# Splitting x without its row factors, in a hybrid attention and retention layer

## The chip, the cores and the metric

One core of a Trainium2 chip runs the whole layer. The metric is device time of one execution in microseconds (us). TensorE multiplies matrices, VectorE, ScalarE and GpSimd work on elements, SyncE issues all DMA transfers. The pages of the profile call them PE (its weight loads PEld), DVE, ACT, POOL and SP (SPq where it issues a transfer).

## What is computed

x is 2048 rows by 1024 columns of float32. The reference, shortened (the chunk-wise retention is given in its effect: sums over decayed keys inside a chunk, a state R across chunks):

```python
h = x * rsqrt(mean(x*x, axis=-1) + 1e-6) * norm_gain      # one factor per row, one gain per column
aq, ak, av, ag, rq, rk, rv, rg = split(h @ w_in, SPLIT_POINTS, axis=-1)

# group A: 16 heads of 64, 4 KV heads, window of two chunks of 64 rows
q, k = rms_norm(aq, q_norm_gain), rms_norm(ak, k_norm_gain)      # per head
s = q @ k.T / 8 + bias                                           # ALiBi, band of 128 keys
p = exp(s - m) / (sum(exp(s - m)) + exp(sink - m))
attn = p @ av

# group B: 8 heads, q and k of 64, v of 128, decay g per head
o = ((rq @ rk.T) * dmat) @ rv + (rq * wq) @ R                    # R: g**64 * R + (rk * wk).T @ rv
ret = (o - mean(o)) * rsqrt(var(o) + 1e-6) * ret_norm_gain       # per head and row

mixed = concatenate([attn * silu(ag), ret * silu(rg)], axis=-1)
out = x + mixed @ w_out
```

The projection w_in has 5632 columns, w_out is 2048 by 1024.

## The kernel before

**Tiling.** The rows are taken in four blocks of 512 (BLK, four tiles of 128, t = 0 to 3). A block has four units (NU), one for each KV head: four attention heads with their key and value, and two retention heads. So there are 16 units n, unit 0 to 3 on the first block, and so on. All matrix products are made of float32 operands that are split in two, high + low, with three matmuls for each pair (high x high, high x low, low x high; `mm3` and `job`, L1327 to L1329). A high half is a copy that rounds (ScalarE), a low half is the original minus the high half.

**Jobs of TensorE.** Unit n has jobs (n,0) to (n,19). Jobs 0 to 3 are q, k and v of a row tile (24 matmuls with 384 columns, panel 0 of the weights), 4 and 5 the attention gate, 6 and 7 retention q and k (24 matmuls with 512 columns each, weights stationary, so the result has features as rows: panel 1), 8 to 11 retention v and gate of a row tile (panel 2), 12 to 19 the output projection (12 matmuls with 512 columns each, panel 3), done while the next unit starts. Results land in three PSUM banks jb in turn; job m waits until the reader of the job three before has freed its bank. Between the jobs stand short pieces: TQ(n,t) transposes the normed q and k of a tile, S_ makes scores, PT transposes probabilities, PV multiplies with v, A and I are the retention products, MT transposes the mixed result, XB (L1443) transposes the row factors of x.

**x.** A transposed tile of x (features as rows) comes from DRAM into one of two buffers xt (x_turned, L253). For it the row factor is needed along the columns: xsq (ScalarE, a sum of squares from a row-major copy: acc in the first block), xms_ (VectorE, L1028, mean and eps), xpow (GpSimd, L401, power -0.5), XB (TensorE, one factor column spread over 128 and transposed). h (VectorE, L1042) scales xt in place by gain and factor, eight instructions of 128x128 per tile; in block 0 the factor is read from the PSUM bank of XB, later from xrb in SBUF (buffer rawqn). xh (ScalarE, L648) makes the high halves hTH, two copies of 128x512 per tile. The low halves hTL come from VectorE in block 0 (xl_first, through `sub`, L804) and from GpSimd in later blocks (xl, L408). For block b + 1 h of the first two tiles stands in the middle of the last unit of block b, the rest of it at that unit's end. x_turned of tile t waits for the low halves of tile t - 2, whose buffer it takes.

**Weights.** In the first block a panel is read in four pieces of 128 x 2 slices (load q) into three stages; wh1 (ScalarE, L508) makes each slice's high half, wl1 (GpSimd, L360) the low half; both halves are saved to scratch in DRAM and later blocks reload them (reload), without splitting. SyncE issues each piece's load when the low halves of the piece three before are done, and that piece's save right behind it.

**After the jobs.** qkv (ScalarE) copies the q, k, v bank to raw. VectorE and GpSimd norm q and k (rpow, L367, is the power). ag and agg are the attention gate: tanh from the bank (ScalarE), then (tanh + 1) x bank on VectorE (L914) into gate, which frees the bank. rq_decay, rk, rvg, kw_am (L959, L960), rl and rupd (L979) are retention, gna, gnv, gnb the group norm, mix, mixh, mixl, mtl the mixed result, add the residual. carry_in brings keys and values of the block before, negates the sinks (L820) and copies the retention state rst to rcur.

**Order.** Each engine runs a list of such calls, written out by hand for every unit; semaphores alone order the engines among each other. The start of the lists of TensorE and GpSimd:

```python
XB(0, 0)
job(0, 0); job(0, 1); TQ(0, 0); job(0, 2); TQ(0, 1); S_(0, 0); job(0, 3); job(0, 4); TQ(0, 2)
...
xpow(0, 0); wl1(0, 0, 0); wl1(0, 0, 1); wl1(0, 0, 2); wl1(0, 0, 3); xpow(0, 1); wl1(0, 0, 4)
```

## Time and profile before

| | before |
|---|---|
| median of 3 runs | 1612.38 us (1612.09 to 1613.59) |
| the profiled execution | 1613.94 us |
| its span, first to last instruction | 1612.1 us |
| mean granted clock of TensorE | 0.995 |
| TensorE busy | 1571.5 us of the span |
| VectorE / ScalarE / GpSimd busy | 1139.9 / 654.8 / 482.8 us |
| DMA | 324.67 MB, mean 201 GB/s |

The profile is of one execution. The granted clock is a share of TensorE's full clock, 1.00 for 2.4 GHz and 0.50 for 1.2 GHz. Busy time is time in which an instruction of the engine runs; matmuls are pipelined, so two that follow each other overlap in the rows, and the distance of their starts is what one costs. A wait is shown in front of the instruction that it held up, with what ended it. Durations of single instructions are in us in the timeline and in ns where a row says so.

### The profile page before, as it was taken

What the parts mean: (1) busy time and instruction counts of PE and PEld (TensorE: products, weight loads), DVE (VectorE), ACT (ScalarE), POOL (GpSimd) and SP (SyncE); (2) the same over time, 40 slices, a digit from 0 to 9 for tenths busy, and PEclk for the clock granted to TensorE, in tenths of its full rate; (3) what the DMA queues carried; (4) which work ended last, traced back from release to release, by engine and by line L of the source; (5) the groups of instructions that cost most, each with busy time, mean ns of one, the idle gap of its engine ahead of it and who ended that gap; (6) DMA issues with size and microseconds to landing.
All of it is one profiled execution on the core that took longest, in us unless ns stands there. A gap on an engine that the chain in (4) does not pass through costs nothing.

```text
span 1612.1 us, 24573 instructions
## 1 busy us (share of the span) xinstructions
PE 1571.5 (97%) x8208; PEld 1370.7 (85%) x8208; DVE 1139.9 (71%) x3040; ACT 654.8 (41%) x1892; POOL 482.8 (30%) x477
## 2 busy tenths in 40 slices
PE   4999999999899999999999999999999999999998
PEld 4897888988789889898888988889898898988887
DVE  6798686796965757568694775857788575675864
ACT  4655455454433434333443342433343343333430
POOL 4564675655512022120421202122140211202210
PEclk9999999999999999999999999999999999999999
DMA  8776766774855536445357444546356554353451
GB/s 287 263 274 239 273 251 245 261 258 152 302 213 200 195 118 245 159 158 219 126 227 264 176 175 166 187 162 234 133 195 217 188 219 176 121 214 120 182 209 53
DMA packets 123020, 324.67 MB, mean 201 GB/s; under 512 B 16784, under 2 KB 57872, under 8 KB 122896
## 3 DMA queue, kind: packets, MB, share of 16 engines
q1 hardware_dynamic: 122896, 323.10, 55.0%
q8 instruction: 67, 1.10, 0.3%
q14 instruction: 57, 0.47, 0.1%
HBM read 251.75 MB, written 71.30 MB: 200 GB/s over the span
## 4 chain that ended last, share of the span: by engine, by line
PE 78%; DVE 16%; issue 3%; ACT 1%; DMA 1%; POOL 0%; SPq 0%; DVEq 0%; ACTq 0%; POOLq 0%
PE jb L1327 22%; PE jb L1328 22%; PE jb L1329 22%; PE ob L1387 2%; PE ptb L1373 2%; PE s L1364 2%; DVE xt L1042 1%; DVE oraw L1003 1%; PE ob L1346 1%; DVE rawqn L858 1%; DVE qS L867 1%; DVE mixr L931 1%; PE s L1421 1%; DVE rawqn L855 1%; PE s L1422 1%
## 5 line engine op out<-in xcount | busy, mean ns | idle before, releaser
L1327 PE MATMUL jb<-wH,hTH 128*128 128x512 f32 (+1 forms) x1024 | 377.5, 369 | 12.6 <-DVE hTL L804 12.6
L1328 PE MATMUL jb<-wL,hTH 128*128 128x512 f32 (+1 forms) x1024 | 374.2, 365 | 0.0
L1329 PE MATMUL jb<-wH,hTL 128*128 128x512 f32 (+1 forms) x1024 | 373.9, 365 | 0.0
L1327 PEld LDWEIGHTS jb<-wH,hTH 128*128 128x128 f32 x1024 | 194.4, 190 | 32.0 <-DVE hTL L804 12.0
L1329 PEld LDWEIGHTS jb<-wH,hTL 128*128 128x128 f32 x1024 | 194.2, 190 | 20.5
L1328 PEld LDWEIGHTS jb<-wL,hTH 128*128 128x128 f32 x1024 | 194.4, 190 | 18.1
L1327 PE MATMUL jb<-wH,mxH 128*128 128x512 f32 x512 | 208.8, 408 | 0.0
L1327 PE MATMUL jb<-hTH,wH 128*128 128x512 f32 x512 | 201.4, 393 | 0.7 <-POOL wL L360 0.7
L1329 PE MATMUL jb<-wH,mxL 128*128 128x512 f32 x512 | 201.2, 393 | 0.0
L1328 PE MATMUL jb<-wL,mxH 128*128 128x512 f32 x512 | 201.2, 393 | 0.0
L1328 PE MATMUL jb<-hTL,wH 128*128 128x512 f32 x512 | 199.7, 390 | 0.0
L1329 PE MATMUL jb<-hTH,wL 128*128 128x512 f32 x512 | 199.5, 390 | 0.0
L360 POOL TENSOR_TENSOR wL<-stage,wH 128x512 fp32r<-128x512 f32 (+1 forms) x128 | 161.7, 1287 | 73.4 <-ACT wH L508 73.2
L385 POOL TENSOR_TENSOR mxL<-mixr,mxH 128x256 fp32r<-128x256 f32 x64 | 47.2, 737 | 452.8 <-ACT mxH L596 451.7
L551 ACT ACTIVATE sx<-sx,nm 128x128 f32<-128x128 f32 x256 | 99.8, 391 | 191.1 <-DVE d L900 191.1
L367 POOL TENSOR_TENSOR rstd<-ms,mhalf 128x5 f32<-128x5 f32 x64 | 74.9, 1171 | 139.1 <-DVE ms L838 139.1
L1329 PEld LDWEIGHTS jb<-wH,mxL 128*128 128x128 f32 x512 | 96.6, 189 | 21.3
L1329 PEld LDWEIGHTS jb<-hTH,wL 128*128 128x128 f32 x512 | 96.1, 188 | 20.6
L1327 PEld LDWEIGHTS jb<-hTH,wH 128*128 128x128 f32 x512 | 96.2, 188 | 19.6 <-POOL wL L360 1.1
L1328 PEld LDWEIGHTS jb<-hTL,wH 128*128 128x128 f32 x512 | 96.2, 188 | 18.3
L1328 PEld LDWEIGHTS jb<-wL,mxH 128*128 128x128 f32 x512 | 97.1, 190 | 16.6
L1327 PEld LDWEIGHTS jb<-wH,mxH 128*128 128x128 f32 x512 | 96.9, 189 | 16.7
(146 smaller groups left out, 2904.3 us busy)
## 6 DMA issues: line engine op xcount, KB each, us to landing
wH<-scrH SPq DMA_DIRECT2D x144, 512.0 KB, 7.0
wL<-scrL SPq DMA_DIRECT2D x144, 512.0 KB, 7.9
stage<-wp_dram SPq DMA_DIRECT2D x48, 512.0 KB, 6.2
scrH<-wH SPq DMA_DIRECT2D x48, 512.0 KB, 6.1
scrL<-wL SPq DMA_DIRECT2D x48, 512.0 KB, 6.8
wH<-scrH SPq DMA_DIRECT2D x48, 384.0 KB, 5.3
wL<-scrL SPq DMA_DIRECT2D x48, 384.0 KB, 6.6
xt<-xT_dram SPq DMA_DIRECT2D x16, 512.0 KB, 5.9
```

Source lines behind the costliest of these rows:

```text
L360: pool.tensor_tensor(wL[b][:, s, 0:w], stage[:, (at // 2) % STAGES, s % 2, 0:w], wH[b][:, s, 0:w].bitcast(F32), ALU.subtract).then_inc(S[" ...
L367: pool.tensor_tensor(rstd[:, t % 2], ms[:, t % 2], mhalf[:, 0:5], ALU.pow).then_inc(S["s_rstd"], 1)
L385: pool.tensor_tensor(mxL[:, 0:2, cols], mixr[:, :, :], mxH[:, 0:2, cols].bitcast(F32), ALU.subtract).then_inc(S["s_mixl"], 1)
L551: act.activation(v, v, ACT.Exp, bias=nm4[:, t % 2, i:i + 1], accum_out=den[:, t % 2, i:i + 1])
L855: v.tensor_tensor(qn[:, t % 2, 0:320].rearrange("p (h d) -> p h d", d=HD), raw[:, t % 2, 0:320].rearrange("p (h d) -> p h d", d=HD), rstd[ ...
L858: v.tensor_tensor(qn[:, t % 2, 320:384], raw[:, t % 2, 256:320], rstd[:, t % 2, 4:5].broadcast_to([P, HD]), ALU.mult).then_inc(S["s_qn"], 1)
L1327: pe.matmul(o, lh, rh_, start=i == 0, stop=False)
L1328: pe.matmul(o, lh, rl_, start=False, stop=False)
L1329: m = pe.matmul(o, ll, rh_, start=False, stop=i == last)
L1364: m = pe.matmul(s_parts[:, par, hp], qS[:, t % 2, 2 * hp + par], kHL[:, :, win], start=True, stop=True)
L1373: m = pe.transpose(ptb[:, i * P:(i + 1) * P], sx[:, at:at + P], ident[:, :])
L1387: m = pe.matmul(o, v, pT[:, par * 256:(par + 1) * 256].rearrange("p (r q) -> p r q", q=64), start=i == 0, stop=i == 1)
```

## The change

**x.** h is gone; xt stays as it came from DRAM. xh is now eight ScalarE copies of 128x128 per tile, with the column gain as their scale; xl, in all blocks, is eight VectorE instructions per tile (xt x gain - high half, L1083). hTH and hTL so hold x times gain without the row factor. The factor is applied behind the products: as the scale of the raw copy of q, k, v (qkv), of the retention v copy and of the gate's tanh (rvg), as the row scalar of the low half of v, of kw_am and of gnb, and squared with eps in gnv (xe). For jobs 4 and 5, whose result has rows along its columns, a new VectorE instruction agz (L946) multiplies the bank by xrb, the factor spread over all partitions, into gate, and frees the bank; tanh and agg (L951) then work from gate. XB is made once per block, four transposes behind PT of the block's first unit (in block 0 behind job (0,4)), and xrb_copy follows it. xpow makes two columns, the factor and its half; xms_ is three instructions. Retention q, where it appears linearly, stays without the factor; gnv and gnb make up for it. rq_decay waits for the gate as well.

**Retention state.** rcur and its copy are gone, rst is updated in place; the decay of k is a table of two columns instead of 128 (cret has 387 columns, not 513).

**The start.** SyncE issues the norm gains first, then a quarter of tile 0 of x and a quarter of panel 0 in turn; the fourth quarter goes to buffer sx as a fourth stage. TensorE waits for the low halves of x slice by slice. Jobs (0,0) to (0,4) follow each other without a transpose between them. The saves of pieces 0 to 4 come behind the load of piece 7.

**Orders.** TensorE: in units 1 and 4 more output jobs stand between TQ(.,0) and TQ(.,1). VectorE, ScalarE and GpSimd are rearranged in all units; carry_in stands behind the x splits of tile 1 and 2 in unit 0.

The core of the diff; of the lists, each some hundred lines, only the start of TensorE's and its unit 4 are shown:

```diff
-            def h(b, t):
...
-                for k in range(KT):
-                    i = v.scalar_tensor_tensor(out=xt[:, t % 2, k], in0=xt[:, t % 2, k], scalar=ngain[:, k:k + 1],
-                                               in1=factor, op0=ALU.mult, op1=ALU.mult)
...
+            def xl(b, t, c):
+                for k in (2 * c, 2 * c + 1):
+                    v.wait_ge(S["s_xH"], 32 * b + 8 * t + k + 1)
+                    cols = slice(t * P, (t + 1) * P)
+                    v.scalar_tensor_tensor(out=hTL[:, k, cols], in0=xt[:, t % 2, k], scalar=ngain[:, k:k + 1],
+                                           in1=hTH[:, k, cols].bitcast(F32), op0=ALU.mult, op1=ALU.subtract
+                                           ).then_inc(S["s_xL"], 1)
...
+                for k in (2 * c, 2 * c + 1):
+                    act.activation(hTH[:, k, t * P:(t + 1) * P], xt[:, t % 2, k], ACT.Copy, scale=ngain[:, k:k + 1]
+                                   ).then_inc(S["s_xH"], 1)
...
-                act.activation(raw[:, t % 2], bank_of(n, J_QKV + t)[:, 0:384], ACT.Copy).then_inc(S["s_raw"], 1)
+                if n % NU == 0:
+                    act.wait_ge(S["s_xr"], nth(n // NU, 4, t))
+                act.activation(raw[:, t % 2], bank_of(n, J_QKV + t)[:, 0:384], ACT.Copy,
+                               scale=xr[:, n // NU % 2, t, 0:1]).then_inc(S["s_raw"], 1)
...
+            def agz(n, i):
+                v.wait_ge(S["s_job"], JOB_DONE[n, J_AG + i])
...
+                v.tensor_tensor(gate[:, i * 512:(i + 1) * 512], bank_of(n, J_AG + i)[:, :], xrb[:, :], ALU.mult
+                                ).then_inc(S["s_agz"], 1)
...
-                v.scalar_tensor_tensor(out=gate[:, i * 512:(i + 1) * 512], in0=th[:, :], scalar=1.0, in1=bank_of(n, J_AG + i)[:, :],
-                                       op0=ALU.add, op1=ALU.mult).then_inc(S["s_gate"], 1)
+                v.scalar_tensor_tensor(out=gate[:, i * 512:(i + 1) * 512], in0=th[:, :], scalar=1.0,
+                                       in1=gate[:, i * 512:(i + 1) * 512], op0=ALU.add, op1=ALU.mult).then_inc(S["s_gate"], 1)
...
-                v.tensor_tensor(amr[:, :], ab[:, 0:256], cD, ALU.mult).then_inc(S["s_am"], 1)
+                v.scalar_tensor_tensor(out=amr[:, :], in0=ab[:, 0:256], scalar=row, in1=cD, op0=ALU.mult, op1=ALU.mult
+                                       ).then_inc(S["s_am"], 1)
...
-                v.tensor_copy(rcur[:, :], rst[:, u:u + 1].rearrange("p o c -> p (o c)")).then_inc(S["s_rcur"], 1)
...
+            for c in range(4):
+                sp.dma_start(xt[:, 0, 2 * c:2 * c + 2], xT[0, 0, :, 2 * c:2 * c + 2]).then_inc(s_xp[c], 16)
+                load(c)
...
+            for q in range(5):
+                sp.wait_ge(S["s_wl"], 2 * q + 2)
+                save(q)
...
-            job(0, 0); job(0, 1); TQ(0, 0); job(0, 2); TQ(0, 1); S_(0, 0); job(0, 3); job(0, 4); TQ(0, 2)
+            job(0, 0); job(0, 1); job(0, 2); job(0, 3); job(0, 4); TQ(0, 0); XB(0); job(0, 5); TQ(0, 1)
...
-            job(4, 0); I(3, 2); MT(3, 0); job(4, 1); job(4, 2); I(3, 3); TQ(4, 0); MT(3, 1); job(4, 3)
-            job(3, 12); TQ(4, 1); job(3, 13); S_(4, 0); MT(3, 2); job(3, 14); TQ(4, 2); job(3, 15); S_(4, 1)
+            job(4, 0); I(3, 2); MT(3, 0); job(4, 1); job(4, 2); TQ(4, 0); job(4, 3); I(3, 3); MT(3, 1)
+            job(3, 12); job(3, 13); job(3, 14); TQ(4, 1); S_(4, 0); MT(3, 2); job(3, 15); TQ(4, 2); MT(3, 3)
```

SyncE's first issues, before (a row is one instruction or several alike; in brackets the semaphores that it waits for: s_wl counts weight low halves, s_xL low halves of x):

```order
L289 DMA acc<-x_dram 128x1024
L292 DMA ident<-c_ident_dram 128x128
L253 DMA xt<-xT_dram 128x1024
L294 DMA ngain<-norm_gain_dram 128x8x1
L297 DMA stage<-wp_dram 128x2x384 x2
L289 DMA acc<-x_dram 128x1024
L253 DMA xt<-xT_dram 128x1024
L297 DMA stage<-wp_dram 128x2x384
L302 DMA stage<-wp_dram 128x2x384 [waits s_wl]
```

SyncE's first issues, changed:

```order
L315 DMA ngain<-norm_gain_dram 128x8x1
L318 DMA xt<-xT_dram 128x256
L313 DMA stage<-wp_dram 128x2x384
L318 DMA xt<-xT_dram 128x256
L313 DMA stage<-wp_dram 128x2x384
L318 DMA xt<-xT_dram 128x256
L313 DMA stage<-wp_dram 128x2x384
L318 DMA xt<-xT_dram 128x256
L313 DMA sx<-wp_dram 128x768
L263 DMA xt<-xT_dram 128x1024
L299 DMA acc<-x_dram 128x1024
L322 DMA ident<-c_ident_dram 128x128
```

The row-major tile and the identity moved from the front to behind the first two transposed tiles, and no load of panel 0 waits any more.

VectorE near the end of unit 3, where block 1 is prepared, before (xt and rawqn: scaling of the third tile; rv, gg: retention v and gate; kwr, amr: decayed k and scores; oraw: group norm; kwL, aL: low halves):

```order
L1042 SCALAR_TENSOR_TENSOR xt<-xt,ngain,rawqn 128x128 [waits s_xt0,s_xrb]
L1042 SCALAR_TENSOR_TENSOR xt<-xt,ngain,rawqn 128x128 x7
L804 TENSOR_TENSOR rv<-jb,rv 128x2x128 [waits s_rvt]
L950 SCALAR_TENSOR_TENSOR gg<-th,jb 128x256
L959 TENSOR_TENSOR kwr<-ab,cret 128x128 [waits s_al,s_kwl,s_a]
L960 TENSOR_TENSOR amr<-ab,cret 128x256
```

The same place, changed (rst: retention state; rHL its low half):

```order
L1083 SCALAR_TENSOR_TENSOR hTL<-xt,ngain,hTH 128x128 [waits s_xH,s_dve]
L1083 SCALAR_TENSOR_TENSOR hTL<-xt,ngain,hTH 128x128 [waits s_xH] x3
L834 TENSOR_TENSOR rHL<-rst,rHL 128x128 [waits s_rh]
L1038 BN_AGGR mv<-st 128x2 x2
L1040 TENSOR_SCALAR ve<-mv,xe 128x2 [waits s_dve]
L1083 SCALAR_TENSOR_TENSOR hTL<-xt,ngain,hTH 128x128 [waits s_xH] x6
L1000 SCALAR_TENSOR_TENSOR kwr<-ab,xr,cret 128x128 [waits s_al,s_kwl,s_a]
L1004 SCALAR_TENSOR_TENSOR amr<-ab,xr,cret 128x256
```

Where eight scalings stood in one piece, the low halves stand in pieces between retention work, and each waits for ScalarE's high half.

## Rows read from the trace of the kernel before

**Rows 1.** Busy time of each engine over the span, from the page.

```profile
PE 1571.5 (97%) x8208; PEld 1370.7 (85%) x8208; DVE 1139.9 (71%) x3040; ACT 654.8 (41%) x1892; POOL 482.8 (30%) x477
```

**Rows 2.** Stretches: bounds, length, busy PE PEld DVE ACT POOL (instructions), clock, DMA share, GB/s.

```profile
24.00:42.00 18.00, 8.31 (x39) 7.29 (x37) 14.10 (x39) 9.21 (x21) 8.24 (x7) 0.81 0.82 307
42.00:54.30 12.30, 11.60 (x49) 10.21 (x50) 10.47 (x22) 4.60 (x16) 6.50 (x5) 0.86 0.77 299
54.30:118.00 63.70, 63.62 (x348) 56.21 (x347) 54.37 (x119) 39.14 (x106) 39.95 (x37) 1.00 0.74 254
118.00:200.00 82.00, 78.55 (x400) 66.28 (x400) 63.78 (x147) 43.12 (x121) 46.72 (x42) 1.00 0.74 266
200.00:400.00 200.00, 197.49 (x1035) 171.23 (x1034) 154.47 (x387) 103.23 (x280) 114.47 (x103) 1.00 0.63 229
400.00:440.00 40.00, 33.40 (x179) 30.41 (x178) 38.31 (x97) 15.36 (x41) 23.84 (x20) 0.91 0.81 302
440.00:820.00 380.00, 380.00 (x2005) 332.61 (x2004) 258.79 (x719) 144.90 (x433) 79.84 (x85) 1.00 0.51 186
820.00:840.00 20.00, 19.34 (x99) 16.39 (x99) 18.33 (x55) 6.82 (x24) 3.21 (x3) 1.00 0.70 257
```

**Rows 3.** Timeline to 54 us: start, length, engine, line, operation [idle before <-what ended it].

```profile
7.36 2.16 DVE L1042 SCALAR_TENSOR_TENSOR xt<-xt,ngain,ptb 128x128 f32<-128x128 f32 x8 [1.86 <-DMA ngain<-norm_gain_dram]
8.42 1.99 ACT L508 ACTIVATE wH<-stage 128x384 fp32r<-128x384 f32 x4 [3.18 <-DMA stage<-wp_dram]
9.02 4.32 POOL L360 TENSOR_TENSOR wL<-stage,wH 128x384 fp32r<-128x384 f32 x4 [2.80 <-ACT wH L508]
12.54 0.69 PE L1327 MATMUL jb<-wH,hTH 128*128 128x384 f32 x1 [5.73 <-DVE hTL L804]
...
29.50 0.17 DVE L820 TENSOR_SCALAR nsink<-sink 128x2 f32<-128x2 f32 x1 [3.65 <-DMA sink<-sink_logits_dram]
31.88 5.70 POOL L360 TENSOR_TENSOR wL<-stage,wH 128x512 fp32r<-128x512 f32 x4
32.04 0.69 PE L1327 MATMUL jb<-wH,hTH 128*128 128x384 f32 x1 [5.58 <-DVE hTL L804]
...
36.60 0.34 PE L1327 MATMUL jb<-wH,hTH 128*128 128x384 f32 x1
36.77 0.34 PE L1328 MATMUL jb<-wL,hTH 128*128 128x384 f32 x1
...
53.44 0.50 PE L1327 MATMUL jb<-hTH,wH 128*128 128x512 f32 x1 [0.70 <-POOL wL L360]
```

**Rows 4.** SyncE's issues (start, length), then KB and us from issue to landing.

```profile
0.74 0.39 SPq L289 DMA_DIRECT2D acc<-x_dram  x1
...
20.94 0.56 SPq L310 DMA_DIRECT2D qkg<-q_norm_gain_dram  x1
...
24.08 1.29 SPq L262 DMA_DIRECT2D sink<-sink_logits_dram  x2
25.42 0.62 SPq L212 DMA_DIRECT2D stage<-wp_dram  x1
...
stage<-wp_dram SPq DMA_DIRECT2D x4, 384.0 KB, 5.8
...
ident<-c_ident_dram SPq DMA_DIRECT2D x1, 64.0 KB, 3.4
...
ngain<-norm_gain_dram SPq DMA_DIRECT2D x1, 4.0 KB, 5.2
```

**Rows 5.** Timeline near 129 and from 405 to 434 us.

```profile
128.89 0.52 PE L1346 MATMUL ob<-ident,rawqn 128*128 128x128 f32 x3 [2.57 <-DVE kHL L872]
...
405.50 4.27 DVE L1042 SCALAR_TENSOR_TENSOR xt<-xt,ngain,rawqn 128x128 f32<-128x128 f32 x8
406.38 2.72 POOL L360 TENSOR_TENSOR wL<-stage,wH 128x512 fp32r<-128x512 f32 x2
...
433.51 0.87 PE L1346 MATMUL ob<-ident,rawqn 128*128 128x128 f32 x3 [3.74 <-DVE kHL L872]
```

**Rows 6.** Two lines' own durations: ns least/median/most, first and last start.

```profile
L914 DVE SCALAR_TENSOR_TENSOR gate<-th,jb x32: 674/687/689, 55.1 to 1518.2; 128x512 f32<-128x512 f32 x32
...
L367 POOL TENSOR_TENSOR rstd<-ms,mhalf x64: 1167/1168/1256, 22.5 to 1508.5; 128x5 f32<-128x5 f32 x64
```

More of the change, by code:

```diff
@@ L289, in first_rows, with qk_gains, load @@
                 sp.dma_start(acc[:, t], x[0, t * P:(t + 1) * P, :]).then_inc(s_first[t], 16)
+            def qk_gains():
+                for half in range(2):
+                    rows = slice(half * HD, half * HD + HD)
+                    sp.dma_start(qkg[rows, 0:1], q_gain.rearrange("(d o) -> d o", o=1)).then_inc(S["s_qkg"], 16)
+                    sp.dma_start(qkg[rows, 1:2], k_gain.rearrange("(d o) -> d o", o=1)).then_inc(S["s_qkg"], 16)
+            def load(q):
+                (n, p), c = SPLITS[q // 4], q % 4
+                if q >= STAGES + 1:
+                    sp.wait_ge(S["s_wl"], 2 * (q - STAGES) + 2)
+                sp.dma_start(stage_of(q, W_WIDTH[p]), wp[p][n, :, 2 * c:2 * c + 2, :]).then_inc(s_stage(q), 16)
@@ L304, in _ @@
+            attention_constants(0)
+            load(4)
             first_rows(2)
+            load(5)
             first_rows(3)
-            x_turned(0, 2)
-            x_turned(0, 3)
-            for half in range(2):
-                rows = slice(half * HD, half * HD + HD)
-                sp.dma_start(qkg[rows, 0:1], q_gain.rearrange("(d o) -> d o", o=1)).then_inc(S["s_qkg"], 16)
-                sp.dma_start(qkg[rows, 1:2], k_gain.rearrange("(d o) -> d o", o=1)).then_inc(S["s_qkg"], 16)
@@ L312, in _ @@
-            attention_constants(0)
-            panel(0, 1)
+            load(6)
+            load(7)
+            for q in range(5):
+                sp.wait_ge(S["s_wl"], 2 * q + 2)
+                save(q)
             retention_constants(0)
@@ L1047, in xl_first @@
-            def xl_first(t):
-                for half in range(2):
-                    v.wait_ge(S["s_xH"], 2 * t + half + 1)
-                    ks, cols = slice(4 * half, 4 * half + 4), slice(t * P, (t + 1) * P)
-                    sub(hTL[:, ks, cols], xt[:, t % 2, ks], hTH[:, ks, cols]).then_inc(S["s_xL"], 1)
-            xms_(0, 0); h(0, 0); xl_first(0); xms_(0, 1); h(0, 1); xl_first(1); xms_(0, 2)
-            qk_stats(0, 0); v_parts(0, 0); xms_(0, 3); h(0, 2); qk_norm(0, 0); carry_in(0); qk_stats(0, 1)
@@ L1454, in _, with XB @@
[L1454 to L1459 removed]
+            def XB(b):
+                if b == 0:
+                    pe.wait_ge(S["s_ident"], 16)
+                ab_free()
+                ab_user[0] = ("s_xrb", b + 1)
+                for t in range(NT):
+                    pe.wait_ge(S["s_xr"], nth(b, 4, t))
+                    m = pe.transpose(ab[:, t * P:(t + 1) * P], xr[:, b % 2, t, 0:1].broadcast_to([P, P]), ident[:, :])
+                m.then_inc(S["s_xb"], 1)
```

836 lines of the change are left out of this document (421 added, 415 removed).

## The prediction

> **What bounds the kernel now.** I read the page first: TensorE is busy 97% of the span, the other engines 71% and less [rows 1]. So an edit pays only where TensorE waits or where its clock is halved. The table of stretches shows where that is [rows 2]: from 440 to 820 us TensorE is busy 380.00 of 380.00 us, and so it goes on but for short places. Of its idle time, 1612.1 - 1571.5 = 40.6 us, 12.5 lie before its first weight matmul [rows 3], 9.7 from 24 to 42, 0.7 to 54.3, 3.4 from 118 to 200, 2.5 from 200 to 400, 6.6 from 400 to 440 (the switch to the second block of rows) and about 0.65 at each of the two later switches (one row stands for both); some 4 remain, most of it behind the last matmul. Beside it stands lost clock: a mean granted clock of 0.81, 0.86 and 0.91 [rows 2] means half clock (1.2 for 2.4 GHz) for twice the missing share, each time after a stall of several us. From 400 to 440 that costs at most 0.09 x 40 = 3.6 us.
>
> The timeline names what ended these waits [rows 3]. VectorE starts to scale tile 0 at 7.36, when the norm gains land; ScalarE gets the first weights at 8.42; TensorE starts at 12.54. At 29.5 VectorE has stood 3.65 us for the sink logits, issued only at 24.08 [rows 4], with the scaling of tile 2 behind it; TensorE waits 5.58 us for its low half and restarts at half clock. Job (0,4), the first of panel 1, ends at 54.3, its last step after a wait for GpSimd. At 433.51 the wait is for VectorE too, the low half of k, 3.74 us [rows 5], with VectorE busy 38.3 of the 40 us [rows 2].
>
> **The change part by part.**
>
> *Start, to the end of job (0,4).* Tile 0 no longer needs square sum, power, transpose and scaling before its split. SyncE sends the gains, then a quarter of the tile and of panel 0 in turn. The first weight copy waited at 8.42 behind 1.5 MB; now 0.5 MB is ahead. SyncE's issues begin at 0.74 and follow by 0.45; the first weights, third in line, go out at 1.6 and land 3.4 (a 64 KB load) to 5.8 later (the median of 384 KB) [rows 4]: 5.0 to 7.4. I take 6.0, since the queue is empty; the gains, alone in front, took 5.2 and land with them. GpSimd follows 0.6 later at 1.08 each (4.32 for four) [rows 3]: first matmul 7.7, last low half of panel 0 at 15.2, job (0,0) over near 16. Jobs (0,1) and (0,2) take 24 x 0.17 = 4.1 each (the distance of the two matmuls from 36.60) and no longer meet the sink wait, as carry_in comes behind tiles 1 and 2.
>
> What decides is panel 1. Its first load stands behind the issues of tiles 2 and 3, each held by the low halves of the tile two before, and behind the small constants; from the first of these to the end of the load's own issue took 5.1 us, 20.94 to 26.04 [rows 4]. If the 16 low halves of tiles 0 and 1 are done by 13, the load goes out at 18; if GpSimd's splits hold them up to 17, at 22. It lands 3.6 later (near the 64 KB load's 3.4), 1.2 goes to ScalarE's two copies, and then GpSimd needs 8 splits x 1.43 (5.70 for four [rows 3]) + three powers x 1.17 [rows 6] + two short ones, 16.0. With 0.7 for the last triple job (0,4) ends at 39.5 or 43.5 against 54.3; at that point TensorE still owes 1.3 us of transposes and scores that it had done before. Gain 13.5 or 9.5.
>
> The rows speak for the late end. The scaling L1042 with both tensors in SBUF takes 4.27 us for eight from 405.50, while GpSimd's weight splits run from 406.38 [rows 5], against 8 x 0.27 = 2.16 at the start [rows 3], where one input lies in PSUM: 2.1 us lost beside 2.7 us of splits. The new low half reads two SBUF tensors, and at the start 8.6 us of GpSimd splits lie beside the 4.3 us of 16 low halves: done near 6.5 + 4.3 + 8.6 x 0.77 = 17.4. The Trainium skill, "SBUF — State Buffer", "Who interferes with whom", says it harder: a VectorE instruction with two SBUF inputs contends with a GpSimd instruction that reads SBUF, and the later one blocks fully. By the full price the low halves end at 19.7 and the gain is 7; by the row's it is 9.5; if TensorE's order spares them, 13.5. I take the row's, with a little for the bank of job (0,3) that no longer waits: **-10** (-7 to -15).
>
> *Unit 0 after that.* From 54.3 to 118 VectorE is busy 54.4 of 63.7 [rows 2]. Pulled in by 10 us it has the same work, and some 5 us that it had done by 54.3, in less room. **+2** (0 to +6).
>
> *Held copies.* Five scratch copies (4.2 MB, 11 us at the 0.38 MB/us that 307 GB/s at a share of 0.82 make [rows 2]) now follow the loads of panel 1, and panel 2's first load follows them, landing near 46. Job (0,8) wants it split three jobs of 24 x 0.23 = 5.5 us after (0,4), from 57 on. Nothing, while those 11 us last.
>
> *Unit starts 1 to 3.* 5.9 us idle [rows 2], the longest 2.57 at 128.89, TensorE's transposes of k waiting for VectorE [rows 5]. The new order puts more jobs between a first and a second transpose in unit 1. Half of it: **-3** (0 to -6).
>
> *Switch to block 1 (400 to 440).* GpSimd's x splits beside VectorE are gone. VectorE takes them over instead of the scaling: as many instructions, 8 per tile, but all four tiles now fall behind the V jobs, where two were scaled earlier (+2 x 2.2 us). Against that three output jobs of 2.7 us instead of one stand between TQ(4,0) and TQ(4,1), 5.5 us more cover over the 3.74 us wait [rows 5]. **-7** of 6.6 idle + 3.6 clock (-10 to +2).
>
> *Switches to blocks 2 and 3.* The same VectorE load moves late, the blocking by GpSimd goes, and TensorE's order there has no extra cover. 0.65 us each now. **0** (-1.3 to +6).
>
> *Every unit.* agz adds two 128x512 operations of the kind of L914, 0.69 each [rows 6], 1.38 us of VectorE per unit. From 440 to 820 VectorE is busy 259 of 380 [rows 2]: covered by its idle 121 us. If that cover went, 16 x 1.38 = 22 us would show. agz also frees the gate's bank before tanh, so no later than now. The row copy that goes, and the operations that only change form (decay, values, norm), have one price each as before; ScalarE, busy 145 of 380, covers eight small copies per tile in place of two. The projections' wait for the row factors has nothing late in blocks 1 to 3; in block 0 it is inside the first term. TensorE's matmuls are the same in number, and the tail is the same.
>
> Sum: -10 + 2 - 3 - 7 + 0 = **-18 us**. The profiled execution is 1613.94 (span 1612.1); so 1595.9. The median shown, 1612.38, is 1.6 lower: 1594.3, rounded **1594**.
>
> **The rivals.**
>
> *A: VectorE gives the start back.* For it: 54.4 of 63.7 us busy, and the doubled scaling of rows 5 while weights are split. The start gains 7, unit 0 and the next starts give all of it back but 3, the first switch gains 6, the later ones 0: -9, time 1603. The skill's rule, taken at its word, leads here.
>
> *B: nearly all stalls go.* The order is refitted throughout, and VectorE is relieved of the x splits beside it. -15 - 5 - 10 - 1 = -31: 1581. Against it: the waits near 32, 129 and 434 all end on VectorE, whose work grows.
>
> *C: the start does not move.* If the gains, 1024 pieces of four bytes, hold up the queue until 7.4 as now and panel 1 still loads after 24, only the sink wait goes, and VectorE hands that on: within 0.2% of before.
>
> *D: VectorE becomes the bound of every unit (slower).* agz less the removed row copy, 16 x 1.2 = 19, plus 4.4 late at three switches, 13, and half clock after them, up to 3 x 3.6 = 11; against that the start's -10: +33, 1645. It decides once VectorE cannot finish a unit's start in the jobs given; with a load of 68% and no wait of TensorE from 440 to 820 it is far from that. Half of it would do for slower.
>
> **How the numbers follow.** A measurement can tell about 0.2%, 3.2 us, from no change. The forecast, 1587 to 1600, has 0.56; A, 1600 to 1609, 0.25; B, below 1587, 0.12; C 0.04; D 0.03. The range 1584 to 1604 leaves out about 0.2: most of B, half of what A has above its middle, C and D. Faster 0.93, same 0.04, slower 0.03.
>
> **What would show it.** First weight matmul at 7 to 9 us (wrong above 10); panel 1's first load issued at 18 to 22; job (0,4) over by 39 to 45; no VectorE wait for the sink logits. TensorE idle under 28 us in all, and under 3 in the 40 us at the first switch, with granted clock 1.00 there. If idle stands instead at TQ(8,1) and TQ(12,1), the moved split costs; if VectorE's low halves average well over 0.35 in units 0 to 3, A is right. The gate's product should stay at 0.69. If TensorE's busy time rises with no lower clock, all of this argument fails.

## The result, and the profile after

The changed kernel takes 1617.78 us (median of 8 runs, 1615.44 to 1619.61) against 1612.24 (8 runs, 1611.14 to 1613.92) before: a ratio of 1.0034, interval 1.0025 to 1.0043. It is slower by 5.5 us, where 18 less were forecast. The profiled execution took 1619.43 us with a span of 1617.6.

The busy times of the engines over the span, from the page after:

```profile
PE 1575.4 (97%) x8208; PEld 1372.0 (85%) x8208; DVE 1163.5 (72%) x3080; ACT 693.8 (43%) x1989; POOL 454.9 (28%) x453
```

Against [rows 1] VectorE does 23.6 us more, ScalarE 39 more, GpSimd 28 less, as the diff says. TensorE's idle time is 1617.6 - 1575.4 = 42.2 us, where 40.6 were before and under 28 forecast. The same stretches as [rows 2]; two of them cover 200 to 400 us here:

```profile
24.00:42.00 18.00, 11.44 (x45) 9.25 (x45) 12.52 (x42) 11.03 (x24) 16.29 (x14) 0.81 0.98 354
42.00:54.30 12.30, 10.93 (x55) 9.20 (x56) 7.46 (x15) 5.99 (x13) 5.46 (x6) 1.00 0.94 349
54.30:118.00 63.70, 57.93 (x323) 51.16 (x322) 55.16 (x131) 40.10 (x115) 40.59 (x37) 1.00 0.82 311
118.00:200.00 82.00, 77.83 (x381) 64.81 (x379) 63.87 (x138) 41.67 (x112) 42.15 (x38) 0.96 0.59 218
200.00:300.00 100.00, 95.46 (x492) 82.89 (x491) 78.56 (x187) 52.76 (x139) 58.39 (x53) 0.98 0.65 238
300.00:400.00 100.00, 95.61 (x487) 83.04 (x486) 77.55 (x178) 48.72 (x133) 48.52 (x42) 0.97 0.58 206
400.00:440.00 40.00, 38.50 (x223) 35.49 (x223) 35.66 (x100) 23.14 (x67) 18.28 (x17) 1.00 0.60 236
```

At the switch to block 1 (400 to 440 us) idle time fell from 6.6 to 1.5 us and the granted clock is 1.00. But from 54.3 to 118 TensorE is idle for 5.8 us, where it was for 0.1, and from 118 to 400, where it had been idle for 3.4 + 2.5 us at full clock, for 4.2 + 4.5 + 4.4 us, with a clock of 0.96, 0.98 and 0.97.

Stretches of a shifted kernel hold different work. A sharper measure is the end of a job in either trace, taken as the start of its last matmul plus the distance to a next one. Job (0,4) ends at 54.25 before (54.02 + 0.23, the row behind it is the transpose at 54.26) and at 44.16 now (43.93 + 0.23). The table gives such ends against the kernel before, in us (minus is earlier), for the changed kernel and for six of the kernels below:

| end of job | changed | units23_ old_order | splits_ behind_norms | before_ new_order | memset_ split_time_kept | before_ memset_splits | panel1_ early |
|---|---|---|---|---|---|---|---|
| (0,4) | -10.1 | -10.3 | -10.2 | -2.0 | -11.7 | -1.9 | -12.6 |
| (1,0) | -6.4 | -5.8 | -6.0 | -2.0 | -9.8 | -2.4 | -9.1 |
| (1,4) | +1.7 | +0.8 | +3.2 | -2.0 | -12.0 | -6.5 | -1.6 |
| (2,4) | +6.4 | +1.7 | +3.5 | +3.1 | -12.9 | -8.3 | -1.0 |
| (3,4) | +11.7 | +3.5 | +5.2 | +9.0 | -14.8 | -10.0 | +0.9 |
| (4,4) | +7.3 | -0.9 | +1.9 | +8.1 | -24.4 | -20.0 | -6.2 |
| (15,11) | +5.9 | -2.3 | +0.5 | +8.1 | -25.8 | -20.0 | -7.4 |

Each column is one execution. before_new_order has the start of the kernel before, unchanged, and still ends (0,4) 2.0 us earlier, so the absolute ends hold to about 2 us, and the start's gain may be nearer to 8.

Read down the column "changed": the start gives 10.1. Unit 0 behind it gives back 3.7, and the starts of units 1, 2 and 3 take about 8.0, 4.7 and 5.3 more. The first switch gives 4.4, the two later ones together 1.4. The change wins at the start and loses more in the three unit starts of block 0.

Three places of TensorE's timeline after, at the start, in the start of unit 2 and in that of unit 3 (start, length, operation, idle before and what ended it):

```profile
7.41 0.69 PE L1367 MATMUL jb<-wH,hTH 128*128 128x384 f32 x1 [7.41 <-POOL wL L383]
...
240.37 0.52 PE L1386 MATMUL ob<-ident,rawqn 128*128 128x128 f32 x3 [4.54 <-DVE kHL L900]
...
333.49 0.39 PE L1368 MATMUL jb<-wL,mxH 128*128 128x512 f32 x1
333.72 0.39 PE L1369 MATMUL jb<-wH,mxL 128*128 128x512 f32 x1
...
344.00 0.87 PE L1386 MATMUL ob<-ident,rawqn 128*128 128x128 f32 x3 [4.39 <-DVE kHL L900]
344.52 0.78 PE L1367 MATMUL jb<-wH,mxH 128*128 128x512 f32 x1
345.10 0.63 PE L1368 MATMUL jb<-wL,mxH 128*128 128x512 f32 x1
345.53 0.63 PE L1369 MATMUL jb<-wH,mxL 128*128 128x512 f32 x1
```

The two late waits have the form of the one at 433.51 in [rows 5]: before TensorE transposes the next tile, here tile 2, VectorE must have read the bank of tile 1's transpose, and the low half of k (kHL) is the last to read it. Tile 1 had been transposed at 332.92; VectorE came to it at 342.51. Behind the wait matmuls start 0.43 apart (345.10 to 345.53), against 0.23 before it (333.49 to 333.72): the granted clock is 0.50 from 344.0 to 349.4. What VectorE did in between:

```profile
330.87 1.45 DVE L883 TENSOR_TENSOR rawqn<-rawqn,rstd 128x320 f32<-128x320 f32 x1
332.25 1.31 DVE L886 TENSOR_TENSOR rawqn<-rawqn,rstd 128x64 f32<-128x64 f32 x1
333.58 0.42 DVE L1030 TENSOR_TENSOR oraw<-oraw,s 128x256 f32<-128x256 f32 x1
...
335.83 1.30 DVE L866 TENSOR_SCALAR ms<-ss 128x5 f32<-128x5 f32 x1
337.05 0.59 DVE L1047 TENSOR_SCALAR oraw<-oraw,mv,grs 128x128 f32<-128x128 f32 x2
...
338.33 0.22 DVE L872 CAST veven<-vodd 64x128 fp32r<-64x128 f32 x1
338.57 1.22 DVE L876 CAST vcar<-vodd 64x128 fp32r<-64x128 f32 x1
339.80 1.47 DVE L883 TENSOR_TENSOR rawqn<-rawqn,rstd 128x320 f32<-128x320 f32 x1
341.20 1.28 DVE L886 TENSOR_TENSOR rawqn<-rawqn,rstd 128x64 f32<-128x64 f32 x1
342.51 0.98 DVE L895 SCALAR_TENSOR_TENSOR qS<-ob,qkg,qS 64x256 fp32r<-64x256 f32 x2
343.50 0.35 DVE L900 SCALAR_TENSOR_TENSOR kHL<-ob,qkg,kHL 128x128 fp32r<-128x128 f32 x1
```

and GpSimd in the same time:

```profile
330.67 2.80 POOL L383 TENSOR_TENSOR wL<-stage,wH 128x512 fp32r<-128x512 f32 x2 [1.59 <-ACT wH L525]
335.16 0.70 POOL L420 TENSOR_TENSOR grs<-ve,mhalf 128x2 f32<-128x2 f32 x1 [1.69 <-DVE ve L1040]
335.82 1.28 POOL L383 TENSOR_TENSOR wL<-stage,wH 128x512 fp32r<-128x512 f32 x1
337.28 1.17 POOL L390 TENSOR_TENSOR rstd<-ms,mhalf 128x5 f32<-128x5 f32 x1 [0.17 <-DVE ms L866]
338.42 6.43 POOL L383 TENSOR_TENSOR wL<-stage,wH 128x512 fp32r<-128x512 f32 x5
```

The norm product L883 takes 0.49 us where nothing disturbs it, L886 0.22, the small L866 0.17 and the cast L876 0.22. Here six instructions (two of L883, two of L886, one of L866, one of L876) take 1.2 to 1.5 us, and each of the six lies on a weight split of 1.3 us: 6.2 us lost. From tile 0's to tile 1's low half of k in unit 3, VectorE takes 14.1 us in the changed kernel (7.5 of work, 6.2 of such loss, 0.3 idle) and took 7.4 before (5.3 and 2.1). The new list reads tile 0's transpose earlier, so the state update, tile 2's norm and the first part of the group norm (L1030 to L1040) come to lie behind it, between the two. Two tiles' norm products (330.87 and 339.80) now stand between the two low halves, and both among the splits; before it was one.

Unit 1's 8.0 us look different. The one wait there before, 2.57 us for the low half of k at 128.89 [rows 5], is down to 0.59. But between 100 and 165 us TensorE is idle for 7.0 us where it was for 3.5, in six pieces of at most 2.8 us, all ended by VectorE, which is busy for 59.3 of these 65 us; the clock is 0.95.

### The profile page after: what moved, and what is told of

Same layout as the page of the kernel before. It is cut to its first block, busy times and chain, and to the rows that moved or that the text cites. A ratio compares the mean times of both kernels' runs of the same rounds, so it can differ in the third digit from the quotient of the medians.

```text
span 1617.6 us, 24728 instructions
## 1 busy us (share of the span) xinstructions
PE 1575.4 (97%) x8208; PEld 1372.0 (85%) x8208; DVE 1163.5 (72%) x3080; ACT 693.8 (43%) x1989; POOL 454.9 (28%) x453
## 4 chain that ended last, share of the span: by engine, by line
PE 87%; DVE 7%; DMA 2%; POOL 2%; issue 1%; SPq 1%; ACT 1%; ACTq 0%; DVEq 0%; POOLq 0%
PE jb L1367 25%; PE jb L1368 24%; PE jb L1369 24%; PE ob L1425 2%; PE s L1402 2%; PE ptb L1411 2%; PE ob L1386 1%; DMA stage<-wp_dram 1%; PE s L1457 1%; PE s L1458 1%; POOL wL L383 1%; PE s L1460 1%; PE ab L1470 1%; DVE rawqn L883 1%; DMA xt<-x_dram 1%
## 5 line engine op out<-in xcount | busy, mean ns | idle before, releaser
L1368 PE MATMUL jb<-wL,hTH 128*128 128x512 f32 (+1 forms) x1024 | 373.0, 364 | 0.0
L1367 PEld LDWEIGHTS jb<-wH,hTH 128*128 128x128 f32 x1024 | 193.5, 189 | 39.3 <-POOL wL L383 11.6
L1369 PEld LDWEIGHTS jb<-wH,hTL 128*128 128x128 f32 x1024 | 193.3, 189 | 20.4
L1368 PEld LDWEIGHTS jb<-wL,hTH 128*128 128x128 f32 x1024 | 193.7, 189 | 18.1
L1368 PE MATMUL jb<-wL,mxH 128*128 128x512 f32 x512 | 203.5, 397 | 0.0
L1368 PE MATMUL jb<-hTL,wH 128*128 128x512 f32 x512 | 199.7, 390 | 0.0
L1368 PEld LDWEIGHTS jb<-wL,mxH 128*128 128x128 f32 x512 | 98.4, 192 | 17.0
L1368 PEld LDWEIGHTS jb<-hTL,wH 128*128 128x128 f32 x512 | 96.2, 188 | 18.2
```

The lines of the kernel that those rows point to most:

```text
L1367: pe.matmul(o, lh, rh_, start=i == 0, stop=False)
L1368: pe.matmul(o, lh, rl_, start=False, stop=False)
L1369: m = pe.matmul(o, ll, rh_, start=False, stop=i == last)
```

## The experiments

Two theories of the loss stood against each other. **Order:** the new lists for the starts of units put the wrong work between a first and a second tile; the x split and agz are innocent. **Blocking:** VectorE's small instructions are each held by a GpSimd weight split (wl1, the subtraction that makes a low half), and what counts is which of them lie among the splits. A third was that agz or the removed scaling had made VectorE the bound (rival D). Ratios below are to the kernel before, run on the same chip.

### The order of units 2 and 3 put back

units23_old_order: the heads of units 2 and 3 in all four lists as before, the rest of the change kept. VectorE's list (unit 2):

```diff
-v_parts(2, 2); tql(2, 0); rupd(1, 3); qk_norm(2, 2); gna(1, 3); gnv(1, 3); mtl(1, 1); qk_stats(2, 3)
-gnb(1, 3); v_parts(2, 3); qk_norm(2, 3); tql(2, 1)
+rupd(1, 3); v_parts(2, 2); gna(1, 3); gnv(1, 3); qk_norm(2, 2); tql(2, 0); mtl(1, 1); gnb(1, 3)
+qk_stats(2, 3); v_parts(2, 3); add(1, 0); qk_norm(2, 3); tql(2, 1)
```

and TensorE's: `job(2, 2); I(1, 3); TQ(2, 0); MT(1, 1); job(2, 3)` for `job(2, 2); TQ(2, 0); job(2, 3); I(1, 3); MT(1, 1)`.

> The changed kernel with the start of units 2 and 3 (up to the second low half of q and k) in the order of the kernel before, on TensorE, VectorE, ScalarE and GpSimd; the arithmetic stays changed. Theory O (the new order of these starts is what costs: the retention product of the tile before now stands behind job (n,3), so that VectorE's group norm falls between the norms of tiles 1 and 2): the stalls of 4.54 and 4.39 us before the third transpose go, each with the half clock behind it, about -10 us in all, near 1607. Theory V (VectorE has more to do in every start, in any order, and GpSimd's splits hold it up): nothing or up to -2 us, near 1617.

Measured: 1611.53 us (10 runs), ratio 0.9997 (0.9988 to 1.0007). The loss of these two units is gone, and in the table where it was: from (1,4) to (3,4) it adds 2.7 us, not 10.0. The gain, 6.3 us, is less than the 10 that this theory expected, and far more than the 2 of the other. From 200 to 400 us the clock is back at 1.00:

```profile
200.00:400.00 200.00, 194.22 (x1013) 168.39 (x1012) 159.87 (x384) 105.53 (x287) 109.04 (x98) 1.00 0.61 224
```

### The splits moved, the new order kept

splits_behind_norms: GpSimd alone is told to wait with the weight splits of panel 1 in units 2 and 3 until the norms of all four tiles are done.

```diff
+            def hold(n):
+                pool.wait_ge(S["s_qn"], nth(n, 4, 3))
...
-            rpow(2, 2); wl1(2, 1, 0); wl1(2, 1, 1); gpow(1, 3); wl1(2, 1, 2); rpow(2, 3); wl1(2, 1, 3)
+            rpow(2, 2); gpow(1, 3); rpow(2, 3); hold(2); wl1(2, 1, 0); wl1(2, 1, 1); wl1(2, 1, 2)
```

> The changed kernel; in units 2 and 3 GpSimd's eight weight splits of panel 1 wait until VectorE has normed the fourth tile of q and k. Theory C (VectorE's operations with two inputs in SBUF wait for GpSimd's splits, each for the rest of a split of 1.3 us): the four norm instructions of 1.3 to 1.6 us in each start fall to 0.22 and 0.49, the stalls of 4.54 and 4.39 us go, -8 to -10 us in all, near 1608; panel 1 is still in time, since job (2,4) comes 15 us later. Theory O (the order alone): these norms stay behind the group norm and the stall shrinks by no more than 1 us per unit.

Measured: 1611.09 us (10 runs), ratio 0.999 (0.9979 to 1.0001). This repairs the same stalls with VectorE's and TensorE's order untouched: 6.7 us, against 6.3 by the old order (8 to 10 were expected). VectorE's list is the changed one; the same two norm products at the same place now read, from its timeline,

```profile
334.06 0.49 DVE L886 TENSOR_TENSOR rawqn<-rawqn,rstd 128x320 f32<-128x320 f32 x1
334.47 0.22 DVE L889 TENSOR_TENSOR rawqn<-rawqn,rstd 128x64 f32<-128x64 f32 x1
```

and GpSimd's split starts right behind them:

```profile
334.76 7.54 POOL L383 TENSOR_TENSOR wL<-stage,wH 128x512 fp32r<-128x512 f32 x6 [1.06 <-DVE rawqn L889]
```

So both theories were half right. The order decides which instructions meet the splits; the blocking is what they pay. How much VectorE is held in all hardly differs: added up over its rows to 440 us, the time above what the same instruction takes undisturbed is, by an estimate from the traces, some 65 us in the kernel before, 66 in the changed one and 60 here. What differs is whether TensorE waits behind it.

### The new order in the kernel before

before_new_order: the heads of units 2 and 3 of the kernel before written in the changed order; its x path, start and gate as they were.

> The kernel before with the start of units 2 and 3 in the changed kernel's order on the four engines (carrying in stays behind the state's update), arithmetic and everything else as before. Theory O: +4 to +6 us per unit, so about +10 us, near 1622. Theory V: within 2 us of before.

Measured: 1623.75 us (4 runs), ratio 1.0071 (1.0054 to 1.0088), 11.6 us slower; (1,4) to (3,4) costs 11.0 us more than before, as in the changed kernel (10.0). TensorE stops at the same place for the same thing (and for 4.69 us in unit 3, at 340.97):

```profile
237.02 0.52 PE L1350 MATMUL ob<-ident,rawqn 128*128 128x128 f32 x3 [4.68 <-DVE kHL L874]
```

The loss needs neither agz nor the new x path.

### The gate's product removed

no_gate_factor: agz is gone, and tanh and the gate read the bank, as before. It leaves out the row factor of the attention gate.

> The changed kernel without agz: tanh and the gate's product read the bank of the projection again, as in the kernel before, so the attention gate lacks the row factor; everything else is kept. It prices the 32 added operations of 0.69 us. Theory free: VectorE has idle time in units 4 to 15, so these stay as they are, and only units 0 to 3 can gain, by 0 to 2 us. Theory D of the prediction (VectorE bounds every unit): -10 us or more.

Measured: 1617.87 us (4 runs), ratio 1.0038 (1.0023 to 1.0053), against 1617.78 for the changed kernel. VectorE's busy time falls by 20.4 us (1143.1), and the time stays. Rival D has no part in the loss.

### The start: saves, the sink wait, and panel 1

saves_not_held: each piece's save again right behind its load.

```diff
-load(4); ...; load(5); ...; load(6); ...; load(7)
-save(0); save(1); save(2); save(3); save(4)
+load(4); save(0); save(1); first_rows(2); load(5); save(2); first_rows(3); load(6); save(3); load(7); save(4)
```

> The changed kernel with the scratch copies of pieces 0 to 4 issued right behind each load, as before the change. If holding them back matters: panel 1's transfers wait for the copies, its last low half comes 2 to 5 us later than 43, and job (0,4) ends at 46 to 49, while panel 2 lands earlier and the 1.3 us of waits inside job (0,8) go. If not: job (0,4) ends at 44 and the time is within 1 us of the changed kernel.

Measured: 1622.97 us (4 runs), ratio 1.0062 (1.0047 to 1.0077), 5.2 us over the changed kernel. Job (0,4) ends at 50.08, not 44.16. TensorE stands 10.02 us in the start where the changed kernel stands 5.83:

```profile
34.36 0.69 PE L1369 MATMUL jb<-wH,hTH 128*128 128x384 f32 x1 [10.02 <-ACT rawqn L535]
```

ScalarE's copy of the q, k, v bank is late: the row-major tiles and panel 1's pieces, from which it must first make row sums and high halves, are issued up to 6 us later, with saves ahead of them (the second piece of panel 1 at 26.07, not 22.17). Holding the saves is thus worth about 5 us; of the 5.9 us at job (0,4) some 0.7 stand already in front of the first save, with GpSimd's first weight split at 7.08, not 6.36. More was lost at job (0,4) than the 2 to 5 us expected.

start_waits_gone: VectorE's sink wait had not gone but moved. In the changed kernel it reads

```profile
24.85 0.17 DVE L849 TENSOR_SCALAR nsink<-sink 128x2 f32<-128x2 f32 x1 [6.16 <-DMA sink<-sink_logits_dram]
```

and TensorE stands 5.83 us before 29.47 (the raw copy of the bank is late). Here carry_in(0) stands behind the first norm, and ScalarE copies the banks of (0,0) and (0,1) before it makes the high halves of panel 1.

> The changed kernel; VectorE brings in the sinks (its wait of 6.16 us at 24.85) behind the first norm instead of before the row factors of tiles 1 to 3, and ScalarE copies q, k, v of tiles 0 and 1 before the first two weight copies of panel 1 and the third square. Theory S (VectorE is the bound from the start to unit 1, so its idle time in the first 30 us is paid 80 us later): TensorE's wait of 5.83 us before job (0,3) goes; job (0,4) still ends within 2 us of 44.2, since GpSimd's splits of panel 1 set that, but job (1,3) ends 3 to 6 us earlier and the time falls by 3 to 6 us, to about 1613. Rival: panel 1 sets everything, and nothing past job (0,4) moves by more than 1 us.

Measured: 1618.72 us (5 runs), ratio 1.0038 (1.0024 to 1.0052): nothing. Both waits are gone, and job (0,3) ends at 27.76, not 35.25, but job (0,4) at 44.34, not 44.16, and job (1,0) only 0.5 us earlier. Of the two theories it is the rival that holds. TensorE now waits in job (0,4) for GpSimd's splits of panel 1. This queue of splits sets the end of the start, and the two long waits ahead of it were hidden by it.

### Unit 1

unit1_old_order: the order before from job (0,9) to the end of unit 1's head, on all four engines; TensorE keeps the changed kernel's two output jobs, where the kernel before has one, between TQ(1,0) and TQ(1,1).

> The changed kernel with the end of unit 0 (from job (0,9) on) and the start of unit 1 (to the second low half of q and k) in the order of the kernel before on all four engines. Unit 1's start loses 8 us in the changed kernel (job (1,0) ends 6.4 us earlier than before, job (1,4) 1.7 us later). Theory O1 (the rearranged order of these starts, as in units 2 and 3): 5 us or more come back, near 1612. Theory L (VectorE is late from unit 0 on, whatever the order): job (1,4) still ends within 2 us of 160.4 and the time within 2 us of 1617.8.

Measured: 1623.0 us (4 runs), ratio 1.0069 (1.0052 to 1.0086), so 5.2 us slower than the changed kernel. TensorE now waits 5.38 us near 80.8, for the low half of the transposed probabilities, and (1,0) ends 8.8 us later. So the loss lies at the end of unit 0, where TensorE's old order wants this low half some jobs earlier. From (1,0) to (1,4), the head of unit 1 itself, this kernel loses 4.5 us to the kernel before and the changed one 8.1: the run mixes two edits of opposite sign, and does not tell what the old head alone would do. The whole edit is worse, and the expectation that it would help was wrong.

splits_behind_units123: hold(n) of the second experiment in unit 1 as well.

> The changed kernel; in units 1, 2 and 3 GpSimd's splits of panel 1 wait for the norm of the fourth tile. Units 2 and 3 as in the run with these two alone (-6.7 us). If the 8 us that unit 1's start loses come from the same blocking, unit 1 gains 2 to 5 us more, near 1607. If unit 1 loses because VectorE is late from unit 0 on, it gains less than 1 us and the time is 1611.

Measured: 1611.77 us (10 runs), ratio 0.9994 (0.9984 to 1.0003). Holding the splits of unit 1 as well adds nothing to 1611.09, where 2 to 5 us were expected if unit 1's loss came from these splits.

### All repairs together

all_three: the old heads of units 2 and 3, the held splits of units 1 to 3 and start_waits_gone.

> The changed kernel with the old order in the starts of units 2 and 3, the splits of panel 1 behind the norms in units 1, 2 and 3, and the start's waits gone. If the three causes are separate, the gains add up: -6 to -8 for units 2 and 3 (order and splits remove the same stalls and count once), 0 to -4 for unit 1, -3 to -6 for the start: 1600 to 1608, faster than the kernel before by 0.3 to 0.7%. If they are one cause (VectorE's lag), the sum is no more than the largest, 1610.

Measured: 1609.65 us (10 runs), ratio 0.9985 (0.9976 to 0.9994). The old order and the held splits don't add up, since they remove the same stall, and taking the start's waits away was worth nothing alone. 1600 to 1608 was expected if the causes were separate, 1610 if they were one.

panel1_early: on top of it, SyncE loads panel 1's first piece ahead of the third transposed tile of x and two more right behind it, and ScalarE and GpSimd split the first ones right behind panel 0.

```diff
-load(4); ...; load(5); ...; load(6); ...; load(7)
+load(4); x_turned(0, 2); load(5); load(6); first_rows(1); load(7); x_turned(0, 3)
+qk_gains(); attention_constants(0); first_rows(2); first_rows(3)
```

> On top of the run with all three remedies: panel 1's loads go out between tile 1 and tile 2 of x, and ScalarE and GpSimd split it right behind panel 0. GpSimd's eight splits then lie near 15 to 28, so job (0,4) ends at 34 to 37 instead of 44.4. If TensorE is what unit 0 waits for, job (1,0) and all that follows comes 5 to 8 us earlier, near 1603. If VectorE bounds unit 0 and 1, job (1,0) moves, but job (1,4) stays within 2 us of 159.3 and the time within 2 us of 1609.7.

Measured: 1606.24 us (5 runs), ratio 0.9959 (0.9946 to 0.9972). The first load goes out at 10.42, not 21.06, and job (0,4) ends at 41.64, 2.5 us earlier (7 to 10 were expected). It is the fastest kernel that computes the whole layer, 6 us under the kernel before.

panel1_early_units23: panel1_early without the hold of unit 1.

> The run with the early panel 1, without holding unit 1's splits behind its norms. If the blocking costs unit 1 anything: slower than 1606.2 by 1 to 3 us. If unit 1 loses for VectorE's lag from unit 0 alone: the same or up to 1 us faster, since panel 1 of unit 1 is split earlier.

Measured: 1609.59 us (10 runs), ratio 0.998 (0.9971 to 0.999). By the medians the hold in unit 1 is worth 3.3 us here, where it was worth nothing on the changed kernel, but the two intervals (0.9946 to 0.9972, 0.9971 to 0.999) just meet. Whether it depends on the rest, and why, was not settled.

### How much the blocking costs in all

splits_as_memset: GpSimd writes zeros for the low halves of the weights and reads nothing; the low half of every weight is left out of the result.

```diff
-pool.tensor_tensor(wL[b][:, s, 0:w], stage_of(at // 2, w)[:, s % 2], wH[b][:, s, 0:w].bitcast(F32), ALU.subtract)
+pool.memset(wL[b][:, s, 0:w].bitcast(F32), 0.0)
```

> The changed kernel, but GpSimd's low halves of the weights are a memset of zeros that reads nothing (the low x weight products are computed with zeros). It prices all that the splits do to VectorE and to the start. Theory C (blocking by the splits is the common cause of the losses in units 0 to 3): VectorE's norms have no instance over 1 us in units 0 to 3, the stalls of the starts of units 1 to 3 fall from about 20 us to under 4, and with the start no longer waiting for the splits of panel 1 the time is 1590 to 1598. If VectorE's own work is what is too much: stalls of 8 us or more remain in the starts of units 1 to 3.

Measured: 1584.44 us (one run), 33 us less. But a memset takes 0.53 us, not 1.3, so GpSimd also had more time. Therefore memset_split_time_kept: three memsets in a row for each split (two full, one of a quarter), each waiting for the one before; the same low halves are left out.

> The changed kernel with each low half of the weights written by memsets again, but as many of them in a row as fill the time of a split (two of the full width and one of a quarter; 1.2 to 1.6 us instead of the single memset's 0.50). If the gain of 33 us came from the blocking of VectorE, it stays but for what the later panel 1 costs: job (0,4) again near 44, VectorE's norms without instances over 1 us, the time 1586 to 1594. If it came from GpSimd having less to do: most of it goes and the time is 1605 or more.

Measured: 1587.72 us (one run). GpSimd is now busy for 302 of the first 820 us against 311, and still 30 of the 33 us are gone. VectorE's norm product, all 64 of it (ns least, median, most; first and last start), is never held, though 11 of the 64 start while a memset runs:

```profile
L886 DVE TENSOR_TENSOR rawqn<-rawqn,rstd x64: 477/491/494, 32.2 to 1485.9; 128x320 f32<-128x320 f32 x64
```

against this in the changed kernel:

```profile
L883 DVE TENSOR_TENSOR rawqn<-rawqn,rstd x64: 477/491/1607, 33.7 to 1517.6; 128x320 f32<-128x320 f32 x64
```

What costs is the split as an instruction, which reads two tensors, not how long GpSimd is busy. From 200 to 400 us TensorE is busy nearly throughout:

```profile
200.00:400.00 200.00, 199.69 (x1052) 174.51 (x1051) 143.66 (x410) 109.01 (x302) 100.38 (x205) 1.00 0.64 236
```

before_memset_splits: the same memset (one, 0.50 us) in the kernel before, with the same low halves left out.

> The kernel before with one memset in place of each low half of the weights, as in the run of the changed kernel that took 1584.4 us. It tells what the change itself brings once VectorE is not blocked. Theory C: the change is worth 10 us or more there (the start), so 1595 to 1602 here, and the prediction's ledger was right but for the blocking. If it is 1585 to 1588: the change brings nothing even unblocked, and the whole gain of the memsets is the splits' own.

Measured: 1593.91 us (one run). So a memset for each split takes 18 us off the kernel before and 33 off the changed kernel. Of the 33, 30 are the blocking, by the run with GpSimd's time kept; for the kernel before that was not run, so 18 is at most what the blocking costs it. With memsets the change is worth 1593.9 - 1584.4 = 9.5 us less time; with the splits, 5.5 us more. The low halves of the weights are zeros in these three kernels. That makes TensorE's matmuls no shorter: the 1024 that multiply the low half of the weights by the high half of x take 364 ns on average in the changed kernel (L1368) and in memset_split_time_kept (L1371) alike.

## Why the prediction was wrong

**Where it held.** The start came out near its sum: first weight matmul at 7.41 (forecast 7 to 9), panel 1's first load issued at 21.06 (18 to 22), job (0,4) over at 44.16 (39 to 45; the late end, taken by the price of rows 5, was 43.5). That is -10.1 for -10, in part by luck: panel 1's first load took 5.4 us from its issue to ScalarE's copy (21.06 to 26.50) where 3.6 were taken, the low halves of tiles 0 and 1 were done at 16.2, not 17.4, the held copies below are in it, and the traces agree on this end only to 2 us. TensorE's busy time rose by 3.9 us, with a clock of 0.991 for 0.995. The switch to block 1 went as described, 1.5 us idle and clock 1.00, though worth 4.4 us for the 7 forecast. The later switches gave 1.4 for 0. The gate's product (L951) and agz took 0.69 us each, as the row of L914 [rows 6] said, its 22 us of VectorE stayed hidden, and no_gate_factor shows it.

**The step that failed** is *Unit starts 1 to 3*, "-3 (0 to -6)": they cost +18.0. Its reason was a count of TensorE's jobs between a first and a second transpose in unit 1, and for that one wait it was right, 0.59 us for 2.57. It did not look at what VectorE does between these two, nor at units 2 and 3, where TQ(n,0) moved ahead of I(n-1,3), and where tile 2's norm and the group norm so came between tile 0's and tile 1's low half of k, among GpSimd's splits. [rows 5] had the price: the row of L1042 doubled beside GpSimd. I used it in the start, where eight equal instructions stood in one piece, and nowhere else; yet an instruction of 0.2 us that meets a split loses 1.1, so the short ones of the norms are hurt most. units23_old_order and before_new_order put 6.3 us and 11.6 us on the order of units 2 and 3, splits_behind_norms shows that this order costs only through the blocking. That is 10.0 of the 18.0. For unit 1's 8.0 the memset runs show that they go with the splits (from (1,0) to (1,4) memset_split_time_kept gains 2.2 us where the changed kernel loses 8.1), but not by which instructions: holding panel 1's splits there did nothing, so that part stays open.

**The rule.** The Trainium skill, "SBUF — State Buffer", "Who interferes with whom", has VectorE and GpSimd block each other fully. The rows agree for this kernel: 0.22 becomes 1.28 to 1.32 us. The prediction took the 2.1 us lost beside 2.7 us of splits in [rows 5] for a milder price than the rule's, and gave the rule to rival A with 0.25. They are one price. The start of the changed kernel shows it:

```profile
10.74 5.45 DVE L1083 SCALAR_TENSOR_TENSOR hTL<-xt,ngain,hTH 128x128 fp32r<-128x128 f32 x10 [0.19 <-ACT hTH L671]
```

```profile
6.36 6.08 POOL L383 TENSOR_TENSOR wL<-stage,wH 128x384 fp32r<-128x384 f32 x6 [5.52 <-ACT wH L525]
12.39 2.08 POOL L383 TENSOR_TENSOR wL<-sx,wH 128x384 fp32r<-128x384 f32 x2
```

Of these ten low halves three take 1.08 to 1.10 us instead of 0.34, while the splits follow each other until 14.47; they start 1.0 us apart, so each is held for a whole split, and one gets through between two splits. The last six, behind the splits, start 0.26 apart. This chain of equal instructions lost 2.8 us beside 3.7 us of splits, about the 0.77 of [rows 5]; an instruction of 0.2 us loses nearly a whole split. (By its own terms the prediction's full price ends at 6.5 + 4.3 + 8.6 = 19.4, not 19.7; it changes nothing.)

**Unit 0.** +2 was given, and it took 3.7, inside the range of 0 to 6.

**Held copies** were priced at nothing as "those 11 us last". Undone, they cost 5.2 us of the total and 5.9 at job (0,4). The gain is inside the start's -10, which was put down to other causes, chiefly to the load of panel 1 going out earlier. With the saves back in place only its first piece goes out as early (21.77).

**A wait that did not go.** "No VectorE wait for the sink logits" was wrong: it stands at 24.85, and 6.16 us long. It cost nothing, since GpSimd's splits end later than what it delayed.

**The rivals.** A named the right mechanism and side: VectorE gives the start back. Its sign came too: VectorE's low halves average 0.42 us in units 0 to 3, and 0.49 in the start. Its size was too small by 15 us, since it let the unit starts give back only what was gained. D forecast a slower kernel by another way, agz, which is refuted; no rival had "slower" by VectorE's small instructions behind GpSimd. B's 1581 is what splits_as_memset nearly reaches: without the splits nearly all stalls go.

## What to carry to other kernels

Beside the list of each engine, lay the list of GpSimd: a reordering is to be judged by which short VectorE instructions, with a waiting engine behind them, come to lie among GpSimd's two-input instructions. Each that does, and takes its inputs from SBUF, can lose up to one whole GpSimd instruction, however short it is. Where such work has slack, as the weight splits of a panel here, hold it behind the short chain; a wait in GpSimd's list did as much as a change of four lists (6.7 and 6.3 us). And before long waits are removed, ask which queue ends last behind them: 6.2 and 5.8 us of waiting in the start were worth nothing, while issuing panel 1's first load 10.6 us earlier let job (0,4) end 2.5 earlier.
